# Expert outputs of a routed mixture stored by index into token rows, with a changed order of the expert loop

## What is computed

```python
gp = softmax(x @ w_rg + b_rg); g_val, g_idx = top_k(gp, 1)          # 1 of 4 groups
el = (x @ w_re + b_re).reshape(-1, 4, 8)                              # 8 experts a group
e_val, e_idx = top_k(softmax(el[g_idx]), 2)                           # 2 of 8
e_w = e_val / sum(e_val) * g_val
hg = einsum('md,edf->mef', x, w_gate); hu = einsum('md,edf->mef', x, w_up)
act = silu(hg) * hu * combine[..., None]       # combine: e_w at the two picked experts, else 0
y = einsum('mef,efd->md', act, w_down)         # w_gate, w_up (1024 x 256), w_down (256 x 1024)
x = x + y
```

## Time and profile of the kernel before

| | us |
|---|---|
| median of 3 runs (1317.05 to 1318.78) | 1317.66 |
| the profiled execution | 1315.11 |
| its span, first to last instruction | 1313.3 |
| experts of layer 0, TensorE, from the first gathered rows to the last `down` | 373.9 to 638.2 |
| experts of layer 1, likewise | 974 to 1279.7 |

### The profile page before, as it was taken

The page is one execution under the profiler, slowest core; times in us unless marked ns, Lnnn a source line. Parts: engine busy times, 40 slices in busy tenths (PEclk is TensorE's granted clock), DMA queues, the critical chain, the costliest instruction groups (busy, mean ns, idle before and its releaser), DMA issues.

```text
span 1313.3 us, 18788 instructions
## 1 busy us (share of the span) xinstructions
PE 1080.9 (82%) x7117; PEld 685.1 (52%) x7118; DVE 371.8 (28%) x710; ACT 225.7 (17%) x402; POOL 117.7 (9%) x168
## 2 busy tenths in 40 slices
PE   5999998899688767887479989999778778888880
PEld 4886685675354334444157767654354434444440
DVE  2000013442521111011057899352341111111115
ACT  4000101344101000111040101151201101011112
POOL 1000101100010000000122121000011010111003
PEclk9999998999799889899789999999889989899995
DMA  9623116500849999999631100330568997799936
GB/s 381 252 90 141 60 53 136 218 0 37 316 127 416 429 426 428 398 424 428 223 139 65 48 18 1 98 154 32 224 256 356 411 413 278 289 385 408 379 114 228
DMA packets 38895, 304.78 MB, mean 232 GB/s; under 512 B 8416, under 2 KB 8448, under 8 KB 28448
## 3 DMA queue, kind: packets, MB, share of 16 engines
q1 hardware_dynamic: 13616, 242.76, 45.7%
q0 software_dynamic: 8784, 31.48, 6.7%
q10 hardware_dynamic: 16416, 29.45, 6.5%
HBM read 269.85 MB, written 33.83 MB: 231 GB/s over the span
## 4 chain that ended last, share of the span: by engine, by line
PE 53%; DMA 19%; DVE 10%; issue 9%; ACT 4%; DVEq 1%; POOL 1%; ACTq 1%; POOLq 0%
DMA expert_outputs<-ar 16%; PE psum L1425 10%; PE psum L1603 8%; PE psum L1531 6%; PE psum L1658 5%; PE psum L1733 5%; DVE ar L1290 4%; PE psum L1419 3%; PE psum L1695 3%; PE psum L1476 2%; PE psum L1363 2%; PE psum L1492 1%; PE psum L1591 1%; PE psum L1631 1%; DMA ring<-expert_outputs,ix 1%
## 5 line engine op out<-in xcount | busy, mean ns | idle before, releaser
L1603 PE MATMUL psum<-ring,ar 128*64 128x256 f32 x1408 | 159.6, 383 | 2.9 <-DVE ar L1203 2.9
L1603 PEld LDWEIGHTS psum<-ring,ar 128*64 128x64 f32 x1408 | 103.9, 139 | 67.3 <-issue 23.6
L1658 PE MATMUL psum<-ring,ar 128*64 128x512 f32 x352 | 92.5, 649 | 54.6 <-DVE ar L1221 54.6
L1425 PE MATMUL psum<-ar,ring 128*128 128x272 f32 x576 | 132.7, 393 | 0.0
L1214 DVE TENSOR_TENSOR ar<-ar,psum 128x128 f32<-128x128 f32 x64 | 18.4, 288 | 388.4 <-ACT ar L758 388.0
L1733 PE MATMUL psum<-ar,ring 128*128 128x272 f32 x512 | 120.5, 397 | 3.0 <-DVE ar L1276 3.0
L1425 PEld LDWEIGHTS psum<-ar,ring 128*128 128x128 f32 x576 | 109.3, 190 | 22.9 <-issue 0.3
L1733 PEld LDWEIGHTS psum<-ar,ring 128*128 128x128 f32 x512 | 97.7, 192 | 27.8 <-issue 4.2
L1290 DVE SCALAR_TENSOR_TENSOR ar<-ar,sv 128x512 f32<-128x512 f32 x120 | 107.0, 893 | 5.8 <-ACT ar L845 1.9
L774 ACT ACTIVATE ar<-psum 128x512 f32<-128x512 f32 x64 | 38.2, 597 | 285.2 <-DMA expert_outputs<-ar 158.4
L1531 PE MATMUL psum<-ring,ar 128*128 128x512 f32 x192 | 84.1, 594 | 0.0
(11 more groups left out here) (209 smaller groups left out, 1117.2 us busy)
## 6 DMA issues: line engine op xcount, KB each, us to landing
ring<-w_moe SPq DMA_DIRECT2D x44, 3072.0 KB, 15.8
ar<-w_moe SPq DMA_DIRECT2D x20, 3072.0 KB, 16.9
expert_outputs<-ar ACTq DMA_DIRECT2D x128, 128.0 KB, 16.4
ring<-w_mix SPq DMA_DIRECT2D x4, 3072.0 KB, 13.7
ring<-w_pw SPq DMA_DIRECT2D x6, 2048.0 KB, 9.9
ring<-kv_in SPq DMA_DIRECT2D x2, 2880.0 KB, 11.6
expert_outputs<-ring POOLq DMA_DIRECT2D x8, 512.0 KB, 11.6
normed_rows<-ar ACTq DMA_DIRECT2D x8, 512.0 KB, 2.6
```

What stands on the lines that cost most here:

```text
L1425: t = mm(psum[:, b + h, 0:HALF], w[:, k, P * c:P * c + P], hT[:, k, HALF * h:HALF * h + HALF], start=k == 0, stop=k == KD - 1)
L1603: t = mm(psum[64 * f:64 * f + 64, u % 2, 0:2 * P], xt[:, k, 64 * (u % 2):64 * (u % 2) + 64], w[:, k, f, :], start=k == 0, stop=k == KD - 1)
L1658: t = mm(psum[64 * h:64 * h + 64, 4 + u % 2, :], aT[:, 64 * k:64 * k + 64], slot(u)[:, o:o + 512], start=k == 0, stop=k == 1)
```

## The change

- The output store of an expert becomes one indirect DMA from POOL (`outputs`, `chunk_out`) in place of two plain ones from ScalarE. Its destination is the token's own row: `ys_dram` is now 4 x 544 rows of 512 columns, and a token's two outputs lie side by side in 8 KB.
- The table now holds a code for each place, in one form for all 48 jobs: four times the token plus twice the pick plus the half, less an offset for empty rows that puts their index out of bounds. Both indirect DMAs, the gather and the store, get `bounds_check`, so empty rows are skipped both ways. Because skipped rows of `xg` and `xe` are not written, POOL clears these buffers once a layer (four `memset`s). Three instructions of VectorE make the gather indices `tg` from `tb`.
- The ten gathers of the combination become five plain loads from SyncE (`fetch`), 1 MB each for a full tile, each with a semaphore of its own. In layer 0 they are put between the second and the third load of `w_pw1`, and the third load waits for the fourth tile (`fetched[3]`).
- TensorE does `turn_act(u-1)` inside `gate_up(u)`, behind the fifth of its eight steps, and waits for the two halves of `xt` separately; VectorE does `keep_at(u-1)` ahead of the product and of `keep_rows`; no engine drains at the end of a pass.
- POOL's order in an expert `u`: for even `u` the gather of the pair that is needed four pairs on, then `further_rest(u)` (the stores of the chunks of `u`, and the gathers of its second and later chunks), `further_first(u+1)` (the gather of the first chunk of the next expert), then `outputs(u)`, which waits for `y_kept`.
- The zeros at the start and the wait for them are gone.

```diff
-        ys_dram = nc.dram_tensor("expert_outputs", ((EXPERTS + MORE) * JOB, D), F32, kind="Internal").ap()
+        ys_dram = nc.dram_tensor("expert_outputs", (4 * TOK, 512), F32, kind="Internal").ap()
...
-        yg = [ring[:, q // 2, 4096 + D * (q % 2):4096 + D * (q % 2) + D] for q in range(8)] + [xg[0], xg[1]]
+        yg = [ring[:, i, 4096:4096 + 2 * D] for i in range(4)] + [view(M_G, 2 * D)]
...
+            def fetch(n):
+
+                sp.wait_ge(moe.all_out, n + 1)
+                for i in range(TILES):
+                    src = ys_dram.rearrange("(t q) c -> t (q c)", q=4)[P * i:P * i + ROWS[i], :]
+                    sp.dma_start(yg[i][0:ROWS[i], :], src).then_inc(moe.fetched[i], 16)
...
             for c in range(4):
 
+                if c == 2:
+                    fetch(0)
+                    sp.wait_ge(moe.fetched[TILES - 2], 16)
                 sp.wait_ge(moe.down_done, EXPERTS - MSLOTS + (PW1_SLOT[c] - EXPERTS) % MSLOTS + 1)
...
             experts(1)
+            fetch(1)
...
-            nc.gpsimd.memset(ring[:, 3, 0:D], 0.0).then_inc(zeros_made, 1)
...
-                pool.wait_ge(moe.tokens, n + 1)
+                pool.dma_start(spare_dram, cst[0:JOB, C_FOLD:C_FOLD + 32]).then_inc(ex[n].out, 16)
+                pool.wait_ge(moe.places, n + 1)
+                nc.gpsimd.memset(xg[0], 0.0).then_inc(moe.rows_clear, 1)
                 pool.wait_ge(moe.jobs, n + 1)
+                nc.gpsimd.memset(xg[1], 0.0).then_inc(moe.rows_clear, 1)
+                pool.wait_ge(moe.tokens, 3 * n + 3)
+                nc.gpsimd.memset(xg[2], 0.0).then_inc(moe.rows_clear, 1)
...
-                    pool.indirect_dma_start(xg[v], None, xn_dram, bass.IndirectOffsetOnAxis(ixg[:, v:v + 1], 0)
-                                            ).then_inc(moe.rows_in[v], 16)
+                    pool.indirect_dma_start(xg[v], None, xn_dram, bass.IndirectOffsetOnAxis(ixg[:, v:v + 1], 0),
+                                            bounds_check=TOK - 1, oob_is_err=False).then_inc(moe.rows_in[v], 16)
...
+                def further_rest(it, u):
+
+                    chunks, before = counts(it, u)
+                    with pool.If(chunks > 0):
+                        with pool.If(chunks > 1):
+                            with pool.Fori(1, chunks) as c:
+                                chunk_rows(before + c)
+                                chunk_out(before + c - 1)
+                        chunk_out(before + chunks - 1)
+
+                def outputs(it, u):
+
+                    b = u % 3
+                    pool.wait_ge(moe.y_kept, MSLOTS * it + (EXPERTS * n + u + 1))
+                    nc.gpsimd.tensor_copy(ixy[:, b:b + 1], tb[:, bass.ds(MSLOTS * it + u, 1)]).then_inc(moe.iy_ready, 1)
+                    pool.wait_ge(moe.iy_ready, MSLOTS * it + (EXPERTS * n + u + 1))
+                    pool.sem_inc(moe.seen, 1)
+                    pool.indirect_dma_start(ys_dram, bass.IndirectOffsetOnAxis(ixy[:, b:b + 1], 0), yj[b], None,
+                                            bounds_check=4 * TOK - 1, oob_is_err=False).then_inc(moe.y_out[b], 16)
+
+                def body(it, gathers, jobs=MSLOTS, last=False):
+                    for u in range(jobs):
+                        if u % 2 == 0 and gathers:
+                            rows_of(3 * it + (u // 2 + 4), u + 8)
+                        further_rest(it, u)
+                        if not (last and u == jobs - 1):
+                            further_first(it, u + 1)
+                        outputs(it, u)
...
-                def store(job, y, done):
...
-                    for q in range(2):
-                        act.dma_start(rows[:, 512 * q:512 * q + 512], y[64 * q:64 * q + 64, :]).then_inc(done, 16)
...
-                    for u in range(jobs + 1):
-                        if u < jobs:
-                            gate_up(it, u, first)
+                    for u in range(jobs):
+                        if later(first, u):
+                            keep_at(it, u - 1, first)
+                        gate_up(it, u, first)
                         if u % 2 and jobs == MSLOTS:
                             keep_rows(3 * it + (u // 2 + 1))
-                        if u:
-                            keep_at(it, u - 1, first)
+                        if later(first, u):
                             further(it, u - 1)
...
                     for k in range(KD):
+                        if k % 4 == 0:
+
+                            pe.wait_ge(moe.rows_kept, MSLOTS * it + (EXPERTS * n + 2 * (u // 2) + 1 + k // 4))
+                        if k == 5 and later(first, u):
+
+                            turn_act(it, u - 1, first)
```

More of the change, by code:

```diff
@@ L344, in over_experts, with later @@
             body(EXPERTS // MSLOTS, False, EXPERTS % MSLOTS)
+        def later(first, u):
+            return not first or u > 0
         def hT_of(call):
@@ new lines, in further_first @@
+                def further_first(it, u):
+                    chunks, before = counts(it, u)
+                    with pool.If(chunks > 0):
+                        chunk_rows(before)
+                def further_rest(it, u):
+                    chunks, before = counts(it, u)
+                    with pool.If(chunks > 0):
[4 more added lines that the diff above has]
+                        chunk_out(before + chunks - 1)
@@ L1675, in experts @@
                 over_experts(pe, body)
+                last = EXPERTS // MSLOTS, EXPERTS % MSLOTS - 1
+                turn_act(*last, False)
+                further(*last, 1)
+                down(*last, False)
             experts(0)
```

172 lines of the change are left out of this document (83 added, 89 removed).

## The result

The changed kernel is slower by 0.85%, little but clear of the scatter: 1329.20 us median (1328.18 to 1330.60, 4 runs) against 1318.16 us (1317.05 to 1318.78, 4 runs), a ratio of 1.0085 with a 95% interval of 1.0068 to 1.0103. Forecast was 1275. The profiled execution took 1330.22 us with a span of 1328.3, against 1315.11 and 1313.3, so the trace has 15.0 us more of span to explain.

What follows compares the result with a forecast made beforehand. DMA was taken to bound layer 0's experts and TensorE layer 1's. Layer 0's -30 and layer 1's -12.5 made -42.5 on the profiled 1315.1, so 1272.6, as a median 1275; forecast case 1258 to 1292, range 1244 to 1303.

Steps and rivals of the forecast that it cites:

- What bounds the kernel: Layer 0's experts are bound by DMA, 8.68 us per load; stores on q10 are the slowest queue and delay `keep_y`.
- the clue of the pieces: DMA engines take turns among queues piece by piece; a small queue pays per piece, about 0.93 us behind each weight piece.
- Part 1, fewer rows: Layer 0's 26 streamed loads: skipped empty rows shrink stores and gathers, 0.45 us per load; -12 us (0 to -16).
- Part 2, stores to POOL: Layer 0's end: 7.9 turns per expert against 9 offered, so `keep_y` no longer lags; -9 us (0 to -13).
- the rival with 13.5 turns: Slow side: skipped rows still take turns, 13.5 per expert on q0 in both layers; +30 us, 1347, chance 0.11.
- Part 3, order: Layer 1's expert loop: copy and turn hide behind `gate_up`, 12.3 to 12.5 us a pair; -31 us (-28 to -34).
- I leave the 11 us of waits: Layer 1's experts: the 11 us of waits beyond pairs and chunks were kept unchanged, as loads still run beside.
- Part 4, later gathers: Layer 1's chunk rows: gathers issued later, lead 0 to 5 us, landing 7 to 11; +17 us (0 to +35).
- Part 5, head: Start of each layer: clearing a third buffer and two more VectorE instructions, +1.5 us; layer 0 takes it back.
- Part 6, combination: After the experts: layer 0's combination starts 10.3 us after `keep_y`, -9 us (-2 to -12); layer 1, 0 (-2 to +1).
- The rival by whole packets: Engines take turns by whole packets: 22 us per pair instead of 17.4 in layer 0, near 1370 us; chance 0.02.
- the two signs of being wrong: Packets on q0 as many as rows with the empty ones, or landings of stores above 20 us.

Runs made afterwards that it cites:

- before_order: The kernel before with only the new expert loop order on TensorE, VectorE and ScalarE: 1306.32 us, ratio 0.9886.
- ahead_old_order: after_ahead with the loop order of TensorE, VectorE and ScalarE undone, as in the kernel before: 1302.52 us, 0.9872 of the kernel before.
- after_ahead: Changed kernel with each further chunk's gather issued once the previous chunk is turned, the first ahead of the loop: 1277.19 us, 0.9662 of the kernel before.

## Why the prediction was wrong, point by point

**What bounds the kernel**, and the loads of layer 0: right. 8.0 us per load came as forecast (8.0 to 8.3), q0 is below 10% (8.4%), and the clue of the pieces held: with half the piece all waits for stores in layer 0 were gone.

**Part 1, fewer rows** (-12): the last streamed load is issued at 590.71 instead of 600.56, though the first work came 3 us later, so the stream won 12.9 us. That this matches is in part luck. Counted the same way, before_order, which skips nothing, won 4.4 us (last load issued at 598.01, first gather 1.8 us later). And of the reason one half holds: bytes are saved, turns are not.

**Part 2, stores to POOL** (-9): the mechanism failed. The sum of turns, 7.9 per expert, was to be below the 9 offered; it is 8.95, and `keep_y` waits 130.9 us in layer 0 where it waited 118.5. The count was wrong at both ends. Skipped rows keep a packet, which raises it. And a store of 128 rows of 2 KB doesn't take 128 packets: no packet on q0 has 2048 bytes and 1315, gathered rows among them, have 4096, so two 2-KB rows ride in one, full or empty. That lowers it, and is why the rival with 13.5 turns didn't come. The Trainium skill ("DMA: Bandwidth & Descriptors", SWDGE vs HWDGE vs iDMA) gives 4096 B as the preferred size of a packet, and the packet as the point where an engine changes queue; these records agree for q0. The other queues do otherwise: in the kernel before, q10's stores went in packets of 2048 bytes, and a weight load's packets on q1 have 24,576.

The tail gave 5 us, and they belong to part 3. From the issue of the last streamed load to the end of the last `down` of layer 0 it took 37.6 us before and 32.7 after. With the stores on POOL and the old order (ahead_old_order) it took 37.4, with the new order (after_ahead) 32.4. With 16 us for the load, after has 16.7 us left where 12 were named. So part 2 gave as good as nothing of its 9. (What the prediction quotes of the same page of the Trainium skill, "generally faster", stands there in the section Issuing engine by pattern and not in Specifications; no run here compares the engines alone.)

**Part 3, order** (-31): in the changed kernel the 34.2 us are gone from TensorE's waits, and the chain of waits has a pair's `down` 1279.92 - 1267.52 = 12.4 us behind the one before, as forecast:

```profile
1267.52 1.87 PE psum L1708 x8
...
1279.92 1.87 PE psum L1708 x8
```

As a gain of time it is 15.7 us alone and 25 to 28 in after_ahead, of which the `down`s of layer 1 show 9.9 and 14.3. The failed step is "I leave the 11 us of waits": in before_order waits of 12.5 and 9.1 us for turned rows came in place of those removed. And 5 to 6 us of it lie in layer 0, much of it at its end, where I had put nothing.

**Part 4, later gathers** (+17, range 0 to +35): this is the step that failed and turned the sign. The mechanism was named, TensorE behind it too, and the issue order was read rightly. The size was 67.2 us of waits and some 6 of clock. Three things in it were too favourable. The lead was "0 to 5 us" and measured -2.5 to 1.4. The landing was "7 to 11 us", where its own rows had 6.3 to 18.4 and came from a kernel whose gathers had few DMAs ahead of them on q0; with stores on the same queue it was 8.4 to 23.7. And the factor of one half "for the stretches where loads pause" had no row behind it: the loads go on until the slots are full, just while the landing runs (DMA share 0.81 to 0.88 in the five landings). It was not carried through either: 2 x 2.5 + 3 x 4 to 3 x 10 is 17 to 35, and halved 9 to 18, so +17 is the top of the halved sum. Full landings of five chunks are 69.4 us.

**Part 5, head**: right. The first gather of layer 0 is issued at 372.25 instead of 369.21, but 1.45 of these 3.0 us lie ahead of the table, and before_order, whose head is the old one, has such a shift too (1.8 us). From the first table instruction to the gather it is 3.1 us instead of 1.5, 1.6 more. **Part 6, combination** (-9 and 0): -10.0 and -0.8; the first operation of VectorE starts at 633.49, 10.05 us after `keep_y` at 623.44 (forecast 10.3, below 11).

**The sum.** Layer 0 was -30 and measured -24.8. Layer 1 was -12.5 and measured +39.6 in its experts. Had part 4 been 70 instead of 17, the same sum would have given 1328. That it comes so near is in part luck: for the profiled execution it gives 1325.6 where 1330.2 was measured, short by the 5 us that layer 0 missed. With the gathers early, the kernel takes 1277, so the rest of the sum, its errors in parts 2 and 3 included, comes out some 19 us above the 1258 that it would give without part 4, with one wait of 11.6 us still in it. The range failed because its upper bound for part 4, 35 us, came from the rows of a queue that the change itself makes longer. The rival on the slow side had its weight on another cause. The rival by whole packets, with 22 us for a pair in layer 0, is out: a pair took 16.0 us. Of the two signs of being wrong, the packets of skipped rows came. Landings of stores above 20 us came too, but they could tell nothing: on the chain of waits the kernel before had them already, 20.4 to 27.6 us.

## What to carry to other kernels

When stores move to an engine that also issues gathers, write down for each gather what is ahead of it in that engine's program and on its queue, and price it with its landing under the new load, not with the landing read from the old queue. A landing that was hidden by many iterations of lead costs its full length when the lead is gone, five times in this case, and TensorE's clock with it. Give such a gather its own condition (buffer free, one more to come) instead of a place in the loop: that one edit was worth 52 us here, and smaller load pieces beside it took the kernel to 0.951 of the one before.

## What the runs showed of the hardware

- A row that an indirect gather skips still leaves a packet of 4 bytes on the queue: 143.1 packets per load with skipping, 143.8 without. Two skipped 2-KB rows of an indirect store leave one of 8 bytes (632 in 170 us). Only the bytes go.
- An indirect store of 2-KB rows by POOL moved in packets of 4096 bytes, two rows in each, where ScalarE's plain stores of such rows had packets of 2048 bytes (2521 of them among q10's 3149 in 430 to 600 us, the others being completions).
- Halving the pieces of a large load (24 to 12 KB) cost at most 2% of its rate (65.53 MB against 66.80 in the same 170 us; 62.06 against 61.61 in the kernel before) and took away all 130.9 us of waits for stores in layer 0.
- Code in POOL's program that never runs, 4 gathers long for each expert, cost 10.7 us of 1277 (four runs, 6 to 20 us), with 15 instruction packets instead of 3 in 170 us.
- After a wait of 24 us TensorE's granted clock was 0.61 for 10 us of work, and a chunk's `gate_up` took 6.35 us instead of the 3.69 of the next one at a clock of 1.00.
